# Attention and output projection as one pipeline over 24 blocks, with q and k split in the first projection

## The chip, the core and the metric

The kernel runs on one core of a Trainium2 chip. A core has TensorE (PE in the rows; its weight loads are listed apart as PEld), VectorE (DVE), ScalarE (ACT), GpSimd (POOL) and SyncE (SP), each with its own instruction stream. They wait for each other by semaphores. SP and POOL start the transfers between device memory and the two on-chip memories. The metric is the device time in microseconds; the median of the runs shown is what a change is measured against.

## What is computed

One encoder layer on 1024 + 2048 tokens of width 1024, in float32 (24 blocks of 128 tokens, block 8 starts the second sequence):

```python
h = rmsnorm(x, norm_mix)
z = h @ w_in                      # 1280 columns: 512 Fourier, 512 q, 128 k, 128 v
f = fourier_mix(z_f, w_fourier)   # 2-D DFT over positions and channels, then a 128x128 map per group
a = banded_attention(q, k, v)     # 8 query heads, 2 kv heads, 64 wide; keys of the blocks before, here, after
x = x + concat(f, a) @ w_out
h = rmsnorm(x, norm_ffn)
aff = softmax(h @ w_router)       # 16 experts; each takes its top 128 + 256 tokens
x = x + sum over experts of gate * ((silu(h @ w_gate) * (h @ w_up)) @ w_down)
y = rmsnorm(x, norm_final)
```

Attention of one query block: scores of at most 384 keys per head, plus a relative-position bias, softmax with one extra learned logit per head (the sink), times v.

## The kernel before, in words

A float32 product is made of three float32r products: each operand is split into a high part (a rounded copy, made by ACT) and a low part (operand minus high part, made by DVE), and `three_pass` (lines 103 to 107) adds hi·hi, hi·lo and lo·hi in PSUM. Where `pe.matmul` or `pe.transpose` is given plain float32, it is used whole; the trace shows such a matmul as two passes.

The stages run one after the other; between two of them all engines meet at a barrier.

1. `mixer_in` normalises x, multiplies by w_in in 6 chunks of 512 tokens, and stores z transposed (`zT`) and v by rows, both as float32.
2. `fourier` leaves f in the on-chip buffer `f_sb`, and stores it into `mixT`, in part from the next stage.
3. `attention` loops over the blocks. SP loads q and k of the next block, as float32. ACT makes their high parts (L771, L772), DVE q's low part (L818), and POOL k's low part (L733). q's high and low part lie one above the other on 128 partitions; a head's scores are one matmul with 128 rows (k_hi twice, L885) and one with 64 rows (k_lo, L886). DVE adds the bias and takes the maximum (L826), ACT takes the exponentials (L780), DVE divides (L847), PE transposes the probabilities in tiles of 128 keys (L897), ACT copies them out of PSUM (L762), PE multiplies by v (L904, 64 output rows, both kv heads into PSUM rows 0 to 63). The head outputs go to `mixT` in device memory. w_out is loaded and split beside this.
4. `mixer_out` loads each block of `mixT`, splits it (L1024, L1052), multiplies by w_out (48 matmuls of 512 columns a block), adds x (L1063), normalises (L1031 to L1070), stores h2 as a high and a low row of 4 KB each, transposes the block (L1106) and multiplies by the router weights (L1114). The logits are stored to device memory.
5. `routing` loads the logits and picks the tokens by a bisection on DVE.
6. `experts` loops over 16 experts, at 97 to 98 us each. Per expert, PE does the gate and up products (384 matmuls of 384 columns), transposes the gathered rows of the next expert, high and low part apart (L1611, 48 transposes of float32r), and does the down products (144 matmuls of 512 columns). ACT and DVE only copy the two transposed parts out of PSUM (L1472, L1517).
7. `final_norm`.

The order on each engine is written out by hand. Three limits matter below: PSUM has 8 banks of 512 columns; a waiting instruction holds up all that stand behind it on its engine; ACT, DVE and PE hand over to each other several times for each block.

Of the kernel before, what the change touches and what calls it, by code (L numbers as in the profile page):

```python
# [22 lines left out]
F32 = mybir.dt.float32  # L23
F32R = mybir.dt.float32r
# [7 lines left out]
P = 128  # L32
# [118 lines left out]
class SplitWeights:  # L151

    PIECES = 4

    def __init__(self, nc, kept, w):
        def sem(name):
            return kept.enter_context(nc.semaphore(f"wo_{name}"))

        self.KW = KT // self.PIECES
        self.raw = kept.enter_context(nc.sbuf_tensor("wo_raw", [P, 2, self.KW, D], F32))  # L160
        self.hi, self.lo = (kept.enter_context(nc.sbuf_tensor(f"wo_{n}", [P, KT, D], F32R)) for n in ("hi", "lo"))
        self.view = w.rearrange("(k p) n -> p k n", p=P)
        self.arrived, self.hi_done, self.lo_done = [sem("in0"), sem("in1")], sem("hi_done"), sem("lo_done")

    def load(self, sp, i):
        if i >= 2:
            sp.wait_ge(self.lo_done, i - 1)
        sp.dma_start(self.raw[:, i % 2], self.view[:, i * self.KW:(i + 1) * self.KW]).then_inc(self.arrived[i % 2], 16)

    def split_hi(self, act, i):  # L170
        act.wait_ge(self.arrived[i % 2], 16 * (i // 2 + 1))
        act.activation(self.hi[:, i * self.KW:(i + 1) * self.KW], self.raw[:, i % 2], ACT.Copy).then_inc(self.hi_done, 1)

    def split_lo(self, dve, i):
        ks = slice(i * self.KW, (i + 1) * self.KW)
        dve.wait_ge(self.hi_done, i + 1)
        dve.tensor_tensor(self.lo[:, ks], self.raw[:, i % 2], self.hi[:, ks].bitcast(F32), ALU.subtract).then_inc(self.lo_done, 1)

def mixer_in(nc, x, w_in, g_mix_cols, ident_d, rel_bias, bucket_rows, toeplitz, zT, v_rows):
# [4 lines left out]
    GRP = ZT + 1  # L186
    WP = 4
    ctx, sb, sem, ps = scope(nc, "p1")
    with ctx:
# [11 lines left out]
        z_sb = sb("z", [P, GRP, CW])  # L201
# [9 lines left out]
        zT_v = zT.rearrange("(t p) (c n) -> c t p n", p=P, n=CW)  # L211
        v_v = v_rows.rearrange("(c j p) d -> c p j d", p=P, j=CH)
        w_v = w_in.rearrange("(k p) n -> p k n", p=P)
        KW = KT // WP

        @block.sync
        def _(sp):
            sp.dma_start(ident[:, :], ident_d).then_inc(const_in, 16)
            sp.dma_start(g_col[:, :], g_mix_cols).then_inc(const_in, 16)
            bias_rows.load(sp, rel_bias, bucket_rows)  # L220
            for i in range(WP):
                if i >= 2:
                    sp.wait_ge(w_lo_done, i - 1)
                sp.dma_start(w_raw[:, i % 2], w_v[:, i * KW:(i + 1) * KW]).then_inc((w_in0, w_in1)[i % 2], 16)
            bias_rows.store(sp, toeplitz)
            with sp.Fori(0, NCH) as c:
                for g in range(GRP):
                    if g % 2 == 0:
                        sp.wait_ge(z_act, c * 5 + (g // 2 + 1))
                    else:  # L230
                        sp.wait_ge(z_dve, c * 5 + (g // 2 + 1))
                    if g < ZT:
                        sp.dma_start(zT_v[c, g], z_sb[:, g]).then_inc(stored, 16)
                    else:
                        sp.dma_start(v_v[c], z_sb[:, g].rearrange("p (j n) -> p j n", j=CH)).then_inc(stored, 16)
            sp.wait_ge(stored, 16 * GRP * NCH)
            sp.wait_ge(bias_rows.stored, 16)
# [9 lines left out]
        def _(act):  # L247
# [8 lines left out]
            def body(c, last):  # L256
# [5 lines left out]
                for g in range(0, GRP, 2):  # L262
                    if g == 0:
                        act.wait_ge(stored, c * (16 * GRP))
                    act.wait_ge(m_done, c * GRP + (g + 1))
                    act.activation(z_sb[:, g], ps[:, 4 + g % 4], ACT.Copy,
                                   scale=DH ** -0.5 if FW <= g * P < FW + QW else 1.0).then_inc(z_act, 1)
# [12 lines left out]
        def _(dve):  # L280
# [8 lines left out]
            def body(c, last):  # L289
# [7 lines left out]
                for g in range(1, GRP, 2):  # L297
                    if g == 1:
                        dve.wait_ge(stored, c * (16 * GRP))
                    dve.wait_ge(m_done, c * GRP + (g + 1))  # L300
                    dve.tensor_scalar(z_sb[:, g], ps[:, 4 + g % 4], DH ** -0.5 if FW <= g * P < FW + QW else 1.0,
                                      None, ALU.mult).then_inc(z_dve, 1)
# [15 lines left out]
        def _(pe):  # L318
# [3 lines left out]
            with pe.Fori(0, NCH) as c:  # L322
# [8 lines left out]
                for g in range(GRP):  # L331
                    bank = 4 + g % 4
                    if g < 4:
                        if g == 0:
                            pe.wait_ge(z_act, c * 5)
                            pe.wait_ge(z_dve, c * 5)
                    elif g % 2 == 0:
                        pe.wait_ge(z_act, c * 5 + (g - 4) // 2 + 1)
                    else:
                        pe.wait_ge(z_dve, c * 5 + (g - 4) // 2 + 1)  # L340
# [277 lines left out]
def attention(nc, zT, v_rows, attn_sink, ident_d, toeplitz, w_out, f_sb, mixT):  # L618

    ctx, sb, sem, ps = scope(nc, "p3")
    with ctx:
        ident = sb("ident", [P, P])
        bias = sb("bias", [P, NH, BAND])
        sink = sb("sink", [P, NH])  # L630
        q_raw, k_raw = sb("q_raw", [2 * DH, NH, P]), sb("k_raw", [2 * DH, NKV, BAND])
        q_split = sb("q_split", [2 * DH, NH, P], F32R)
        k_hi, k_lo = sb("k_hi", [2 * DH, NKV, BAND], F32R), sb("k_lo", [DH, NKV, BAND], F32R)
        v_sb = sb("v", [P, 3, KVW])
        s_sb, probs = sb("s", [P, NKV, GH, BAND]), sb("probs", [P, NKV, GH, BAND])
        mx, nm, es, esum, rs = (sb(n, [P, NKV, GH]) for n in ("mx", "nm", "es", "esum", "rs"))
        den = sb("den", [P, NKV, GH])
        gate = sb("gate", [P, NKV, GH])
        pt_sb = sb("pt", [P, NKV, 3, GH * P])
        o_sb = sb("o", [DH, NKV, GH * P])  # L640
        const_in, bias_in = sem("const_in"), sem("bias_in")
        f_stored = sem("f_stored")
        v_in, s_mm, added, t_mm, pt_done, pv_mm, o_out = (
            sem(n) for n in ("v_in", "s_mm", "added", "t_mm", "pt_done", "pv_mm", "o_out"))
        qk_hi_done, q_lo_done, k_lo_done = sem("qk_hi_done"), sem("q_lo_done"), sem("k_lo_done")
        qk_in, den_done = [sem(f"qk_in{kv}") for kv in range(NKV)], sem("den_done")
        stat, exp_done, normed = sem("stat"), sem("exp_done"), sem("normed")
        stored = [sem(f"stored{k}") for k in range(NKV)]
        block = ctx.enter_context(nc.Block())
        qT = zT[FW:FW + QW].rearrange("(h p) n -> p h n", p=DH)  # L650
        kT = zT[FW + QW:ZW].rearrange("(h p) n -> p h n", p=DH)
        o_v = mixT[FW:].rearrange("(v h p) (b n) -> v b p h n", v=NKV, p=DH, n=P)

        schedule, b = [], 0
        for s in SEQS:
            n = s // P
            final = b + n == TT  # L660
            schedule += [(b, b + 1, 2, 2 if b else 0, 3, 1, 0), (b + 1, b + 2, 3, 2, 3, 0, 0), (b + 2, b + n - 2, 3, 3, 3, 0, 0),
                         (b + n - 2, b + n - 1, 3, 3, 2, 0, 0), (b + n - 1, b + n, 2, 3, 0 if final else 2, 0, 1)]
            b += n

        def over_blocks(eng, body):


            for first, end, tiles, prev, after, at_start, next_at_start in schedule:
                lead, coming = 1 - at_start, (after, 1 - next_at_start)
                if end - first == 1:  # L670
                    body(first, tiles, prev, coming, lead)
                else:
                    with eng.Fori(first, end) as blk:
                        body(blk, tiles, prev, coming, lead)

        def wait(eng, sem_, value):
            if not isinstance(value, int) or value > 0:
                eng.wait_ge(sem_, value)


        N0 = SEQS[0] // P
        f_store_at = {0: 0, 1: 1, N0 + 1: 2, TT - 1: 3}

        def pieces(b, lag):

            at = {N0 - 2: (0,), N0 - 1: (1,), N0: (2,), TT - 2: (3,)}
            return at.get(b - lag, ()) if isinstance(b, int) else ()

        def split_cols(b):
            return slice(0, 2 * P if isinstance(b, int) and b == 0 else BAND)  # L690

        @block.sync
        def _(sp):
            sp.dma_start(ident[:, :], ident_d).then_inc(const_in, 16)
            sp.dma_start(sink[:, :], attn_sink.partition_broadcast(P)).then_inc(const_in, 16)
            def load_qk(b, tiles, lead):
                for kv in range(NKV):
                    wait(sp, q_lo_done, (b - 1) * NKV + kv + 1)
# [1135 lines left out]
```

## Time and profile before

| | |
|---|---|
| median of 3 runs | 3316.39 us (3312.01 to 3317.18) |
| profiled execution | span 3313.0 us from its first to its last instruction; no other time of it is given |
| PE busy | 2969.1 us, 90% of the span |
| DVE, ACT, POOL busy | 45%, 38%, 9% |
| first SP instruction of `attention` | 636.67 us |
| attention from the first score | 654 to 1096 us |
| output projection, from its first matmul to its last logits | 1113 to 1445 us |
| first SP instruction of `routing` | 1447.24 us |
| experts, first transposed row to last down product | 1546 to 3240 us |

Read the shares by stage: in the output projection and in the experts PE has no gap, in attention it has, and in the routing PE is nearly empty. "PEclk" is the share of full speed (2.4 GHz) that TensorE was granted: 1.00 is 2.4 GHz, 0.50 is 1.2 GHz, and a value between is a mean over a stretch that holds both.

### The profile page before, as it was taken

The page shows a single profiled execution, that of the slowest core. Times are in us where ns is not written, and L with a number is a line of the kernel's source. Part 1 is how long each engine was busy: PE and PEld are TensorE (multiplying, and loading weights), DVE is VectorE, ACT ScalarE, POOL GpSimd, SP SyncE. Part 2 cuts the span into 40 slices and gives each one's busy share as a digit, 9 for nine tenths or more (in the row PEclk, how much of TensorE's full clock was granted, in tenths as well). Part 3 has the DMA queues.
Part 4 walks back from the last instruction along what each step waited for, and adds up shares of the span by engine and source line. Part 5 has one row for each costly group of instructions (what it writes and reads, how often), then busy time and mean ns, then how long its engine had stood idle before and what let it go on. Part 6 is the DMA issues. An engine that isn't in the chain of part 4 may idle for free. (4 is left out here: it accounts for less than half of the span.)

```text
span 3313.0 us, 44990 instructions
## 1 busy us (share of the span) xinstructions
PE 2969.1 (90%) x15831; PEld 2527.0 (76%) x15831; DVE 1483.9 (45%) x2921; ACT 1248.4 (38%) x2103; POOL 308.5 (9%) x256
## 2 busy tenths in 40 slices
PE   7999968687899799944999999999999999999990
PEld 5888867543344588834999999999999999999990
DVE  3122147365555344456454444544444444544334
ACT  3121134365566233311343443433433443433334
POOL 0000000011111000000111111111101111111100
PEclk9999988888889899966999999999999999999995
DMA  5121124233222455542455455554545544555428
GB/s 164 64 85 73 42 79 139 65 99 105 79 82 85 135 192 196 195 155 83 157 174 184 143 161 171 177 160 143 177 157 173 183 146 149 174 184 153 151 78 302
DMA packets 252956, 464.88 MB, mean 140 GB/s; under 512 B 12491, under 2 KB 97644, under 8 KB 243180
## 3 DMA queue, kind: packets, MB, share of 16 engines
q1 hardware_dynamic: 225980, 367.71, 32.0%
q0 software_dynamic: 26928, 96.55, 11.3%
q8 instruction: 28, 0.46, 0.1%
q14 instruction: 20, 0.16, 0.0%
HBM read 358.11 MB, written 106.10 MB: 140 GB/s over the span
## 5 line engine op out<-in xcount | busy, mean ns | idle before, releaser
L1162 DVE TENSOR_TENSOR we_lo<-we_raw,we_hi 128x1024 fp32r<-128x1024 f32 x384 | 467.4, 1225 | 626.0 <-ACT we_hi L1157 625.4
L105 PE MATMUL p_psum<-p_xT_hi,we_hi 128*128 128x384 f32 x2048 | 692.9, 338 | 0.0
L107 PE MATMUL p_psum<-p_xT_hi,we_lo 128*128 128x384 f32 x2048 | 685.3, 335 | 0.0
L106 PE MATMUL p_psum<-p_xT_lo,we_hi 128*128 128x384 f32 x2048 | 685.0, 334 | 0.0
L1157 ACT ACTIVATE we_hi<-we_raw 128x1024 fp32r<-128x1024 f32 x384 | 400.0, 1051 | 6.0 <-DMA we_raw<-w_gate 5.8
L106 PEld LDWEIGHTS p_psum<-p_xT_lo,we_hi 128*128 128x128 f32 x2048 | 384.7, 188 | 0.6
L105 PEld LDWEIGHTS p_psum<-p_xT_hi,we_hi 128*128 128x128 f32 x2048 | 384.3, 188 | 0.6
L107 PEld LDWEIGHTS p_psum<-p_xT_hi,we_lo 128*128 128x128 f32 x2048 | 384.4, 188 | 0.0
L105 PE MATMUL p_psum<-we_hi,p_hid_hi 128*128 128x512 f32 x768 | 300.0, 391 | 0.0
L107 PE MATMUL p_psum<-we_hi,p_hid_lo 128*128 128x512 f32 x768 | 299.0, 389 | 0.0
L106 PE MATMUL p_psum<-we_lo,p_hid_hi 128*128 128x512 f32 x768 | 298.9, 389 | 0.0
L1501 ACT ACTIVATE p_y<-p_psum,p_gate_cur 128x512 f32<-128x512 f32 x96 | 66.0, 688 | 348.4 <-PE p_psum L107 217.5
L1476 ACT ACTIVATE p_hid_hi<-p_hid 128x384 fp32r<-128x384 f32 x128 | 67.2, 525 | 340.7 <-DVE p_hid L1564 340.7
L1486 ACT ACTIVATE p_sg<-p_psum 128x384 f32<-128x384 f32 x128 | 63.0, 493 | 287.7 <-PE p_psum L107 287.5
L1448 POOL DMA_INDIRECT x_left<-p_y,p_idx_cur x48 | 83.1, 1731 | 939.9 <-issue 862.2
L105 PE MATMUL p_psum<-p_h_hi,p_w_hi 128*128 128x512 f32 x432 | 169.2, 392 | 0.0
L106 PE MATMUL p_psum<-p_h_lo,p_w_hi 128*128 128x512 f32 x432 | 168.5, 390 | 0.0
L107 PE MATMUL p_psum<-p_h_hi,p_w_lo 128*128 128x512 f32 x432 | 168.3, 390 | 0.0
L105 PE MATMUL p_psum<-wo_hi,p_m_hi 128*128 128x512 f32 x384 | 155.2, 404 | 14.5 <-DVE p_m_lo L1052 14.5
L107 PEld LDWEIGHTS p_psum<-we_hi,p_hid_lo 128*128 128x128 f32 x768 | 144.1, 188 | 30.2
L106 PEld LDWEIGHTS p_psum<-we_lo,p_hid_hi 128*128 128x128 f32 x768 | 144.2, 188 | 29.6
L105 PEld LDWEIGHTS p_psum<-we_hi,p_hid_hi 128*128 128x128 f32 x768 | 144.1, 188 | 29.3
(213 smaller groups left out, 4610.8 us busy)
## 6 DMA issues: line engine op xcount, KB each, us to landing
we_raw<-w_gate SPq DMA_DIRECT2D x32, 2048.0 KB, 7.7
we_raw<-w_up SPq DMA_DIRECT2D x32, 2048.0 KB, 8.0
we_raw<-w_down SPq DMA_DIRECT2D x32, 2048.0 KB, 8.5
h<-p_h_split SPq DMA_DIRECT2D x24, 1024.0 KB, 3.9
zT<-p_z SPq DMA_DIRECT2D x54, 256.0 KB, 2.0
p_x<-x POOLq DMA_DIRECT2D x6, 2048.0 KB, 8.3
p_q_raw<-zT SPq DMA_DIRECT2D x96, 128.0 KB
p_m_raw<-mixT SPq DMA_DIRECT2D x24, 512.0 KB, 5.0
```

What stands on the lines that cost most here:

```text
L105: pe.matmul(out, lhi, rhi, start=first, stop=False)
L106: pe.matmul(out, lhi, rlo, start=False, stop=False)
L107: return pe.matmul(out, llo, rhi, start=False, stop=last)
L1157: act.activation(self.hi[:, n % self.HL, ks], self.raw[:, n % self.RAW, ks], ACT.Copy).then_inc(self.hi_done, 1)
L1162: dve.tensor_tensor(self.lo[:, n % self.HL, ks], self.raw[:, n % self.RAW, ks], self.hi[:, n % self.HL, ks].bitcast(F32), ALU.subtract).th ...
L1448: pool.indirect_dma_start(out=x2[half], out_offset=bass.IndirectOffsetOnAxis(ap=idx_cur[:, st:st + 1], axis=0), in_=y[:, st, :], in_offset ...
L1476: act.activation(hid_hi[:, half * FT + j], hid[:, j % 2], ACT.Copy).then_inc(hid_hi_done, 1)
L1486: act.activation(sg[:, j], ps[:, j, :SLOTS], ACT.Silu).then_inc(sg_done, 1)
L1501: act.activation(y[:, st], ps[:, 4 * half + st], ACT.Copy, scale=gate_cur[:, st]).then_inc(y_done[half], 1)
```

## The change

`mixer_in` writes q and k already split: ACT evacuates the high part of each of the 5 q and k tiles of a chunk, DVE the low part, and both go to device memory (`qk_parts`), 15 stores a chunk in place of 10.

`attention` and `mixer_out` become one function, `mixer`, without loops. Its steps s = -1 to 26 handle four blocks at a time: scores of block s+1, transposes and values of block s, the w_out products of block s-1, the norm and the transposes (`columns`) of block s-2, the router of block s-3. Scores are now two matmuls of 128 rows for each head (k_lo is loaded on both halves, too), in two PSUM banks in turn. The values of kv head 0 go to PSUM rows 0 to 63, those of kv head 1 to rows 64 to 127, and from there, split, straight into the w_out product; w_out's rows are reordered on the host to suit. x, h2 and others lie in `f_sb`, so ACT waits at its start until f of the second sequence is stored. 1/sqrt is taken as exp of a logarithm, x2 and h2 are stored by POOL, and the logits stay on chip for the routing.

h2 is one float32 row of 4 KB. The experts transpose it once (24 transposes of float32 in place of 48 of float32r), and the split is made from PSUM: ACT the high part, DVE the low part behind it.

```diff
@@ mixer_in, vector
+                for g in range(FG, ZT):
+                    dve.wait_ge(z_act, c * ACT_OUT + (FG // 2 + g - FG + 1))
+                    dve.scalar_tensor_tensor(out=qk_lo[:, g - FG], in0=ps[:, 4 + g % 4], scalar=scale_of(g),
+                                             in1=qk_hi[:, g - FG].bitcast(F32), op0=ALU.mult, op1=ALU.subtract).then_inc(z_dve, 1)
@@ mixer, sync: before the loop over blocks
+            load_qk(0)
...
+            load_qk(1)
+            load_v(0)
+            for i in range(2):
+                load_w(i)
+            load_f(0)
+            for g in range(FG):
+                store_f(sp, f_sb, f_stored, fT, 1, g)
@@ mixer, scalar
+            act.preload_act_table_set("natural_log_exp_and_others")
+            act.wait_ge(f_stored, 16 * FG)
+            act.wait_ge(eps_set, 1)
+            for s in STEPS:
+                if here(s):
+                    exps(s, 1)
+                if here(s - 1):
+                    heads_hi(s - 1)
+                if here(s):
+                    pt_out(s, 0)
+                if here(s - 2):
+                    norm(s - 2)
+                if here(s + 1):
+                    exps(s + 1, 0)
+                if here(s):
+                    pt_out(s, 1)
+                    channels_hi(s)
+                if here(s - 2):
+                    columns_out(s - 2, 0)
+                if here(s) and tiles[s] == 3:
+                    pt_out(s, 2)
+                if here(s - 2):
+                    columns_out(s - 2, 1)
@@ mixer, tensor
+                    pe.matmul(out, q_split[:, b % 2, h], k_hi[:, b % 2, kv, keys], start=True, stop=False)
+                    pe.matmul(out, q_split[:, b % 2, h], k_lo[:, b % 2, kv, keys], start=False, stop=True).then_inc(s_mm, 1)
...
+                    last = pe.matmul(ps[kv * DH:(kv + 1) * DH, 4], v_sb[:, b % 2, i, kv * DH:(kv + 1) * DH], pt_sb[:, i, kv],
+                                     start=i == 0, stop=i == tiles[b] - 1)
...
+            for s in STEPS:
+                scores(s + 1, (0, 1))
+                if here(s - 1):
+                    values(s - 1, tiles[s - 1] - 1)
+                    products(s - 1, 0, 0)
+                if here(s - 3):
...
+                    router(s - 3)
+                scores(s + 1, (2, 3))
+                if here(s):
+                    transposes(s, 0)
+                if here(s - 1):
+                    products(s - 1, 1, 0)
+                scores(s + 1, (4, 5))
+                if here(s):
+                    transposes(s, 1)
+                    values(s, 0)
+                if here(s - 1):
+                    products(s - 1, 0, 1)
+                if here(s - 2):
+                    columns(s - 2, 0)
+                scores(s + 1, (6, 7))
+                if here(s) and tiles[s] == 3:
+                    transposes(s, 2)
+                    values(s, 1)
+                if here(s - 1):
+                    products(s - 1, 1, 1)
+                if here(s - 2):
+                    columns(s - 2, 1)
@@ experts, vector
-                    dve.wait_ge(t_mm, e * (2 * KT) + 2 * k + 2)
-                    dve.tensor_copy(xT_lo[:, k], ps[:, (2 * k + 1) % 8, :SLOTS]).then_inc(x_lo_done, 1)
+                    dve.wait_ge(x_hi_done, e * KT + k + 1)
+                    dve.tensor_tensor(xT_lo[:, k], ps[:, k, :SLOTS], xT_hi[:, k].bitcast(F32), ALU.subtract).then_inc(x_lo_done, 1)
```

On PE, a stretch of the attention stage before: the four heads of one kv head (p_q_split is the weight, p_k_hi and p_k_lo stream), then the transposes of the probabilities and the values.

```order
L885 MATMUL p_psum<-p_k_hi,p_q_split 128x384
L886 MATMUL p_psum<-p_k_lo,p_q_split 128x384
L885 MATMUL p_psum<-p_k_hi,p_q_split 128x384
L886 MATMUL p_psum<-p_k_lo,p_q_split 128x384
L885 MATMUL p_psum<-p_k_hi,p_q_split 128x384
L886 MATMUL p_psum<-p_k_lo,p_q_split 128x384
L897 MATMUL p_psum<-p_ident,p_probs 128x128 x8
L904 MATMUL p_psum<-p_pt,p_v 64x512 x2
```

The same engine after the change, at the start of a step in the second sequence: two heads of the next block, the last values of the block before, and its first products with w_out (p_f_hi and p_f_lo are the Fourier channels, f_sb is the room that holds h2T).

```order
L940 MATMUL p_psum<-p_k_hi,p_q_split 128x384
L941 MATMUL p_psum<-p_k_lo,p_q_split 128x384
L940 MATMUL p_psum<-p_k_hi,p_q_split 128x384
L941 MATMUL p_psum<-p_k_lo,p_q_split 128x384
L961 MATMUL p_psum<-p_pt,p_v 64x512 x2
L105 MATMUL p_psum<-p_w_hi,p_f_hi 128x512
L106 MATMUL p_psum<-p_w_lo,p_f_hi 128x512
L107 MATMUL p_psum<-p_w_hi,p_f_lo 128x512
```

What stood in a stage of its own, the products, now stands between the links of attention's chain: 12 such rows follow each group of scores or values.

On DVE, attention before: the maximum of two heads (L826 with its read of the accumulator), the statistics (L836, L837), the normalisation of the block half behind (L844 to L847), and q's low part.

```order
L826 ISA p_s,p_mx<-p_psum,p_bias,p_sink 128x384
L826 ISA p_mx 128x1
L825 MEMSET p_gate 128x1
L826 ISA p_s,p_mx<-p_psum,p_bias,p_sink 128x384
L826 ISA p_mx 128x1
L836 TENSOR_SCALAR p_nm<-p_mx 128x4
L837 TENSOR_TENSOR p_es<-p_sink,p_mx 128x4
L844 TENSOR_TENSOR p_den<-p_rs,p_esum 128x4
L845 RECIPROCAL p_den<-p_den 128x4
L847 TENSOR_SCALAR p_probs<-p_s,p_den 128x384 x4
L818 TENSOR_TENSOR p_q_split<-p_q_raw,p_q_split 64x512
```

After, in the middle of a step: the statistics of block s+1, the logits of block s-3, the norm of block s-2 (L871 to L882, which waits for ACT), and then the next two heads of block s+1.

```order
L840 TENSOR_SCALAR p_nm<-p_mx 128x4
L841 TENSOR_TENSOR p_es<-p_sink,p_mx 128x4
L887 COPY lg<-p_psum 128x16
L871 TENSOR_SCALAR p_var<-p_ssq 128x1
L875 TENSOR_TENSOR p_newton<-p_rstd 128x1
L876 TENSOR_TENSOR p_newton<-p_newton,p_var 128x1
L877 TENSOR_SCALAR p_newton<-p_newton 128x1
L878 TENSOR_TENSOR p_rstd<-p_rstd,p_newton 128x1
L882 SCALAR_TENSOR_TENSOR f_sb<-f_sb,p_rstd 128x1024
L832 ISA p_s,p_mx<-p_psum,p_bias,p_sink 128x384
L832 ISA p_mx 128x1
```

The low part of q is gone, and the norm, which stood in the later stage, now stands ahead of the heads 4 and 5.

## Rows read from the trace of the kernel before

**Rows 1.** Busy time by stage: window, length, each engine's busy us, PEclk, DMA share, GB/s

```profile
654.00:1096.00 442.00, 378.76 (x1200) 180.11 (x1200) 251.55 (x1011) 266.25 (x713) 77.09 (x94) 0.87 0.31 90
...
1113.00:1450.00 337.00, 328.18 (x1719) 279.71 (x1717) 144.55 (x288) 103.53 (x144) 0.00 (x0) 0.98 0.52 182
...
1650.00:3112.00 1462.00, 1462.00 (x8591) 1371.16 (x8590) 674.71 (x838) 573.02 (x781) 190.48 (x123) 1.00 0.51 164
...
3240.00:3313.00 73.00, 0.00 (x0) 0.00 (x0) 39.16 (x90) 38.81 (x108) 0.00 (x0) 0.50 0.80 300
```

**Rows 2.** Waits in attention: who waited for whom, us in total, times, longest

```profile
ACT p_q_split L771 <- DMA p_k_raw<-zT: 72.6, 20, 11.7
...
PE p_psum L897 <- ACT p_pt L762: 30.4, 34, 2.6
```

**Rows 3.** PE in attention, in order of time: start, us, line, operation

```profile
1052.22 2.79 PE L904 MATMUL p_psum<-p_pt,p_v 128*64 128x512 f32 x6
1054.94 0.44 PE L885 MATMUL p_psum<-p_k_hi,p_q_split 128*128 128x384 f32 x1
1055.31 0.43 PE L886 MATMUL p_psum<-p_k_lo,p_q_split 64*128 64x384 f32 x1
...
1057.91 1.09 PE L897 MATMUL p_psum<-p_ident,p_probs 128*128 128x128 f32 x8
```

**Rows 4.** PE in the experts, in order of time

```profile
1699.80 0.33 PE L106 MATMUL p_psum<-p_xT_lo,we_hi 128*128 128x384 f32 x1
1699.97 0.33 PE L107 MATMUL p_psum<-p_xT_hi,we_lo 128*128 128x384 f32 x1
```

**Rows 5.** All engines in the output projection, in order of time: router, products

```profile
1333.12 1.85 PE L1114 MATMUL p_psum<-p_wr,p_h2T 128*128 128x16 f32 x16
...
1339.72 0.39 PE L105 MATMUL p_psum<-wo_hi,p_m_hi 128*128 128x512 f32 x1
...
1339.94 0.39 PE L106 MATMUL p_psum<-wo_lo,p_m_hi 128*128 128x512 f32 x1
```

**Rows 6.** PE in the output projection: the transposes of one block

```profile
1343.12 1.04 PE L1106 MATMUL p_psum<-p_ident,p_h 128*128 128x128 f32 x8
```

**Rows 7.** PE at the transposes of the gathered rows of one expert

```profile
2357.03 4.25 PE L1611 MATMUL p_psum<-p_ident,p_xe 128*128 128x128 f32 x48
2361.11 0.46 PE L105 MATMUL p_psum<-we_hi,p_hid_hi 128*128 128x512 f32 x1
```

**Rows 8.** Groups by line and shape, 400 to 1100 us: busy us, mean ns, idle before

```profile
L780 ACT ACTIVATE p_s<-p_s,p_nm 128x384 f32<-128x384 f32 x160 | 96.3, 606 | 5.1 <-DVE p_nm L836 5.1
L826 DVE CUSTOM_DVE_ANT_0 p_s<-p_psum,p_bias,p_sink 128x384 f32<-128x384 f32 x160 | 92.7, 614 | 3.6
...
L762 ACT ACTIVATE p_pt<-p_psum 128x512 f32<-128x512 f32 x136 | 76.2, 589 | 56.8 <-PE p_psum L897 56.8
...
L847 DVE TENSOR_SCALAR p_probs<-p_s,p_den 128x384 f32<-128x384 f32 x160 | 56.3, 416 | 1.4
```

**Rows 9.** Groups by line, 1000 to 1340 us: the norm

```profile
L1070 DVE SCALAR_TENSOR_TENSOR p_h<-p_x,p_rstd,p_gain 128x1024 f32<-128x1024 f32 x16 | 20.6, 1285 | 0.6
...
L1031 ACT ACTIVATE p_junk<-p_x 128x1024 f32<-128x1024 f32 x17 | 18.0, 1061 | 93.1 <-DVE p_x L1063 93.1
```

**Rows 10.** Busy time in stretches of 12 us, columns as in rows 1

```profile
640.00:652.00 12.00, 0.00 (x0) 0.00 (x0) 0.00 (x0) 1.87 (x4) 1.43 (x2) 0.50 0.66 182
...
808.00:820.00 12.00, 6.43 (x15) 3.82 (x16) 9.27 (x35) 3.83 (x8) 1.63 (x2) 0.61 0.52 163
```

**Rows 11.** SP's first instruction in attention

```profile
636.67 0.33 SPq L694 DMA_DIRECT2D p_ident<-identity  x1
```

**Rows 12.** Start of the routing, in order of time

```profile
1447.24 0.33 SPq L1218 DMA_DIRECT2D p_lg<-logits  x1
...
1451.69 0.23 DVE L1237 CAST p_same<-p_ranks 128x128 bf16<-128x128 f32 x1 [0.95 <-DMA p_ranks<-ranks]
```

**Rows 13.** The transposes of line 1611: PE's idle time before them, us and times

```profile
  DMA p_xe<-h,p_idx_next: 15.3, 1
```

More of the change, by code:

```diff
@@ L148, in store, with mixer_in @@
         sp.dma_start(toeplitz.rearrange("h (p n) -> p h n", n=NREL), self.rows[:, :]).then_inc(self.stored, 16)
[L151 to L181, printed above, removed]
+def mixer_in(nc, x, w_in, g_mix_cols, ident_d, rel_bias, bucket_rows, toeplitz, zT, qk_parts, v_rows):
     CH = 4
@@ L657, in attention @@
[L657 to L690, printed above, removed]
+        w_raw = sb("w_raw", [P, 2, KW, D])
@@ new lines, in mixer, with here @@
+        h_mm, h_out, lg_mm, lg_out = (sem(n) for n in ("h_mm", "h_out", "lg_mm", "lg_out"))
+        block = ctx.enter_context(nc.Block())
+        starts = (0, SEQS[0] // P)
+        ends = (SEQS[0] // P - 1, TT - 1)
+        tiles = [3 - (b in starts) - (b in ends) for b in range(TT)]
+        first = [b if b in starts else b - 1 for b in range(TT)]
+        before = [sum(tiles[:b]) for b in range(TT + 1)]
+        NEWTON = 4
+        STEPS = range(-1, TT + 3)
+        VERSIONS = NH * 2
+        def here(b):
+            return 0 <= b < TT
@@ L774, in exps @@
-            def exps(b, kv, tiles, behind):
-                for h in range(GH):
-                    if h == 2 and behind[2]:
-                        pt_out(*behind, range(2))
-                    wait(act, stat, (b * NKV + kv) * 2 + 1)
-                    act.activation(s_sb[:, kv, h, :tiles * P], s_sb[:, kv, h, :tiles * P], ACT.Exp, bias=nm[:, kv, h:h + 1],
-                                   accum_out=rs[:, kv, h:h + 1]).then_inc(exp_done, 1)
-                act.wait_ge(stat, (b * NKV + kv) * 2 + 2)
-                act.activation(esum[:, kv], es[:, kv], ACT.Exp).then_inc(exp_done, 1)
@@ L802, in _, with exps @@
-            split(0, 0)
-            split(0, 1)
-            split(1, 0)
-            over_blocks(act, body)
-            pt_out(TT - 1, 1, 2, range(2))
-            o_evac(TT - 1, 1)
+            def exps(b, half):
+                for h in range(half * HALF, (half + 1) * HALF):
+                    act.wait_ge(stat, (2 * b + half) * 2 + 1)
+                    scores = s_sb[:, b % 2, h, :tiles[b] * P]
+                    act.activation(scores, scores, ACT.Exp, bias=nm[:, b % 2, h:h + 1],
+                                   accum_out=rs[:, b % 2, h:h + 1]).then_inc(exp_done, 1)
+                heads = slice(half * HALF, (half + 1) * HALF)
+                act.wait_ge(stat, (2 * b + half) * 2 + 2)
+                act.activation(esum[:, b % 2, heads], es[:, b % 2, heads], ACT.Exp).then_inc(exp_done, 1)
@@ L864, in _, with add_max @@
-            first_tile = 0
-            for kv in range(NKV):
-                split(0, kv)
-            def band(head, tiles):
-                return bias[:, head, first_tile * P:(first_tile + tiles) * P]
-            over_blocks(dve, body)
-            normalise(TT - 1, 1, 2)
+            def add_max(b, heads):
+                for h in heads:
+                    dve.wait_ge(s_mm, b * NH + h + 1)
+                    if b >= 2:
+                        dve.wait_ge(t_mm, before[b - 1] * NKV)
+                    at = 0 if first[b] < b else P
+                    dve.tensor_tensor_reduce(
+                        out=s_sb[:, b % 2, h, :tiles[b] * P], in0=ps[:, h % 2, :tiles[b] * P],
+                        in1=bias[:, h, at:at + tiles[b] * P], scale=1.0, scalar=sink[:, h:h + 1],
+                        op0=ALU.add, op1=ALU.max, accum_out=mx[:, b % 2, h:h + 1]).then_inc(added, 1)
@@ L874, in _ @@
         @block.tensor
         def _(pe):
-            pe.wait_ge(const_in, 32)
-            def scores(b, kv, tiles):
-                u = b * NKV + kv
-                pe.wait_ge(q_lo_done, u + 1)
-                pe.wait_ge(k_lo_done, u + 1)
-                for h in range(GH):
-                    wait(pe, added, (u - 1) * GH + (h + 1))
-                    out, head, keys = ps[:, h, :tiles * P], kv * GH + h, slice(0, tiles * P)
-                    pe.matmul(out, q_split[:, head], k_hi[:, kv, keys], start=True, stop=False)
-                    pe.matmul(out, q_split[:DH, head], k_lo[:, kv, keys], start=False, stop=True).then_inc(s_mm, 1)
@@ L908, in body, with scores @@
[L908 to L914 removed]
+            def scores(b, heads):
+                if not here(b):
+                    return
+                if heads[0] == 0:
+                    pe.wait_ge(qk_in[b % 2], 96 * (b // 2 + 1))
+                keys = slice(0, tiles[b] * P)
+                for h in heads:
+                    if b * NH + h >= 2:
+                        pe.wait_ge(added, b * NH + h - 1)
+                    out, kv = ps[:, h % 2, keys], h // GH
+                    pe.matmul(out, q_split[:, b % 2, h], k_hi[:, b % 2, kv, keys], start=True, stop=False)
+                    pe.matmul(out, q_split[:, b % 2, h], k_lo[:, b % 2, kv, keys], start=False, stop=True).then_inc(s_mm, 1)
@@ new lines, in transposes @@
+            def transposes(b, i):
+                if i == 0:
+                    pe.wait_ge(normed, (b + 1) * NH)
+                for kv in range(NKV):
+                    done = (before[b] + i - 1) * NKV + kv + 1
+                    if done > 0:
+                        pe.wait_ge(pt_done, done)
+                    for h in range(GH):
+                        last = pe.transpose(ps[:, 2 + kv, h * P:(h + 1) * P], s_sb[:, b % 2, kv * GH + h, i * P:(i + 1) * P], ident[:, :])
+                    last.then_inc(t_mm, 1)
@@ new lines, in columns, with router @@
+            def columns(b, half):
+                if half == 0:
+                    pe.wait_ge(h2_done, b + 1)
+                    if b:
+                        pe.wait_ge(lg_out, b)
+                else:
+                    pe.wait_ge(h_out, 2 * b + 1)
+                for k in range(4):
+                    at = (half * 4 + k) * P
+                    last = pe.transpose(ps[:, 7, k * P:(k + 1) * P], h2_sb[b % 2][:, at:at + P], ident[:, :])
+                last.then_inc(h_mm, 1)
+            def router(b):
+                pe.wait_ge(h_out, 2 * b + 2)
+                for k in range(KT):
+                    last = pe.matmul(ps[:, 7, :NE], h2T[:, k * P:(k + 1) * P], wr[:, k], start=k == 0, stop=k == KT - 1)
+                last.then_inc(lg_mm, 1)
@@ L1166, with routing @@
 PAY = 5
[L1169 removed]
+def routing(nc, lg, ranks_d, ident_d, weights, pos_m, payload, onehot_row):
     ctx, sb, sem, ps = scope(nc, "p5")
```

705 lines of the change are left out of this document (310 added, 395 removed).

## Prediction

> **What bounds the kernel now.** I read the busy time by stage first. In the experts PE is busy for all of 1462 us at clock 1.00, in the output projection for 328.18 of 337 us at 0.98, in attention for 378.76 of 442 us at 0.87 [rows 1]. So only attention has idle time to give, 63.2 us; elsewhere only fewer or shorter PE instructions help. The waits of attention come next: 72.6 us is ACT on the load of q and k, 30.4 us is PE on ACT's copy of the transposed probabilities [rows 2]; the second is a hand-over from PE to ACT and back with nothing to do between. DVE and ACT work 251.55 and 266.25 of the 442 us there [rows 1], so neither bounds. The reader should then look at PE in order of time [rows 3 to 7], start to start, for the price of one instruction.
>
> **The change on PE, piece by piece.** (Start to start, near full clock.)
> - Scores. In attention 128-row and 64-row matmuls alternate, 0.37 us each (1054.94 to 1055.31) [rows 3]; in the experts, where all have 128 rows, one of 384 columns takes 0.17 (1699.80 to 1699.97) [rows 4]. The new ones have 128 rows. Bounds 0.17 and 0.37; I take 0.173, the row with the same shape: 20 blocks x 16 x 0.173 = 55.4, and 4 end blocks of two tiles, 16 x 0.14 each, 9.0.
> - Values: 1052.22 to 1054.94 is 2.72 us for three instructions of two passes each [rows 3], 0.907 an instruction; 68 tiles x 2 = 136 of them, 123.4.
> - Transposes of float32: eight take 1.04 with a latency of some 0.27 in it, so 0.11 each [rows 6]. 544 of probabilities 59.8, 192 of h 21.1.
> - Products: 0.227 each (1339.72 to 1339.94 is 0.22; a block's mean is the bit more) [rows 5]; 24 x 48 make 261.2. Router 1.85 a block [rows 5], 44.4.
>
> Sum 574 us, at clock 1.00; at the projection's 0.98 it would be 586. A full step is 2.8 + 2.6 + 5.4 + 10.9 + 1.9 + 0.9 = 24.5 us. To this come some six changes between kinds of work in a step, among them those to and from the values, which use 64 output columns; no row holds one alone. Eight transposes next to scores and values last 1.09 us, 0.05 more than eight among full-size work [rows 3, 6]; each alternating score costs 0.20 more than the experts' [rows 3, 4]. Between these I take 0.16, nearer to the scores, which change the size of the weight too: 1 us a step, 24 in all; bounds 0 and 1.2 a step.
>
> A place where a rule and the trace can be compared: alternating 128 and 64 rows costs 0.37 against 0.17 [rows 3, 4]. The Trainium skill ("TensorEngine Tiling (Array Packing)", section Key Properties) says "Mode switching requires drain". That agrees with the two rows; and it speaks against the change where the values (128 rows, 64 columns) still stand six times a step between full-size work. By it the 1 us a step stays; without it the sum would be 24 us less.
>
> **The stage as a whole.** Before, attention and projection take 1447.24 - 636.67 = 810.6 us from SP's first instruction to the routing's [rows 11, 12]. After:
> - (a) ACT's first exponential waits until f is stored, and that store stands on SP behind q, k, bias, v, half of w_out and f: 10.6 MB by their shapes. At 182 GB/s [rows 10] that is 58 us, at 300 (the final norm's) [rows 1] 35; I take 44, between. Nothing hides it: behind ACT's wait stand all its exponentials, so DVE and PE wait too, after the scores of two blocks.
> - (b) From there to the first transposes of block 1, latency counts: on ACT three halves of exponentials (4 x 0.606 each) and then a fourth, four splits of 2048 columns of w_out (two Squares' length, 2.1 each), three copies of 0.6, on DVE two normalisations (4 x 0.416), transposes 0.9 [rows 6, 8, 9]: 9.7 + 8.4 + 1.8 + 3.3 + 0.9 = 24, with hand-overs 28. Bounds 20 and 40.
> - (c) The rest of PE's work, 574 less 13 that (a) and (b) hold, and the 24: 585.
> - (d) After the last product: residual, Square 1.06, the rest of the norm 2.4, transposes, copy, router, logits, the meeting of the engines; in part in PE's sum. 8; bounds 4 and 12.
>
> 44 + 28 + 585 + 8 = 665; saved 145.6.
>
> **Why (c) should hold without waits.** I laid a full step of 25.5 us out, in the written order. PE: heads 0, 1 at 0, last values 0.7, products 2.5, router 5.2, heads 2, 3 at 7.1, transposes 0 at 7.8, products 8.7, heads 4, 5 at 11.4, transposes 1 at 12.1, values 13.0, products 14.8, columns 17.5, heads 6, 7 at 18.0, transposes 2, values, products 21.3, columns 24.1. DVE's work in it: 8 x 0.614 + 8 x 0.416 + 6 copies or sums of 512 columns at 0.6 + 1.285 and small ones, about 14 us; ACT's: 8 x 0.606 + 10 copies at 0.589 + 1.06 and small ones, about 13 [rows 8, 9]. With these the probabilities of heads 4 to 7 are normalised at 5.4 and needed at 7.8; the first transposes are copied at 9.9 and their bank is needed at 12.1; h2 is ready at 14.1 and needed at 17.5; heads 4, 5 are off their banks at 15.2 and needed at 18.0. So each hand-over has 2.2 to 3.4 us, and the 30.4 us of PE's wait in attention [rows 2] has products to stand under. Load waits: q and k come a whole block ahead, already split, and ACT's 72.6 us of waiting [rows 2] goes.
>
> **Other edits.** In the experts 48 transposes take 2357.03 to 2361.11, 4.08 us [rows 7]; 24 of float32 at 0.11 take 2.64; 15 x 1.44 = 21.6 saved, since PE has no gap there [rows 1]. DVE's subtraction now follows ACT's copy; 1462 - 674.71 us of DVE idle time covers it. The first gather moves half the bytes: PE waits 15.3 us for it now [rows 13]; between 0 and half (7.7) is saved, I take 2.4, nearer to 0, since the choice of tokens and the start of the transfer don't shrink. The logits' trip: DVE starts in the routing on another load at 1451.69, 4.45 us after the stage's start [rows 12], so 0.4 is saved there. `mixer_in`: a group of 24 products of 512 columns takes PE 5.4 us; one more DVE pass of 0.6 and the added store (0.26 MB, 1.4 us at 182 GB/s) hide beside it; 0, bounds 0 and +3.
>
> **The sum.** 145.6 + 21.6 + 2.4 + 0.4 = 170 less: 3313.0 - 170 = 3143 us of span. The median shown is 3.4 us above the span, so 3146. Its own bounds: (a) -9/+14, (b) -8/+12, the changes of work -24/+5, the clock +12, gather -5/+2; taken together as independent some -30/+30: 3116 to 3176.
>
> **Rivals.**
> 1. The values of the two kv heads overlap. They now go to different halves of the output columns. In a pair, four passes of 0.45 would take the time of three: 68 x 0.45 = 31 us less, 3115; if two, 61 less, 3085. For it: nothing in PE's row depends on the other head. Against it: before, both stood in the same half, so no row shows two halves side by side, and both need all 128 rows. The Trainium skill (the same page and section) says that different tiles can load weights and multiply in parallel, which is this rival. 20 in 100.
> 2. The margins of 2.2 to 3.4 us fail, as a hand-over costs more than its parts (DVE and ACT each have some ten waits in a step, in a fixed order, and one that is late moves the rest). Then what attention had of idle time stays: 63 us more, 3209. For it: attention had the waits though DVE and ACT were idle for 40% of it [rows 1]. Against it: twice as much PE work now stands between the links. 22 in 100.
> 3. The scores stay at 0.37 us in spite of 128 rows, because each loads new weights behind a wait for a bank: 20 x 16 x 0.197 + 64 x 0.11 = 70 more, 3216. Against it: the experts' row is also a new weight each [rows 4]. 6 in 100.
> 4. The change does not do what it says: the two chains block each other, and a step takes 442/24 + 337/24 = 32.5 us as before [rows 1]. Stage time 780 + 30, all but the experts' gain lost: some 3290 to 3315, no change at the upper end. 2 in 100.
> 5. Slower: PE gets short idle stretches in every step and its granted clock falls with them. The stretch 808 to 820, where PE is busy 6.43 of 12 us, has 0.61, between the two levels of 1.2 and 2.4 GHz, the projection without gaps 0.98 [rows 1, 10]. At a mean clock m the 574 us become 574/m; the 170 are gone at m = 574/744 = 0.77; at 0.70 it is 246 more, 3392. Against it: the step has nearly as little idle time as the projection. 3 in 100.
>
> **Numbers.** The forecast has 47 in 100. The range reaches over it to rival 1 with one pass saved and on the other side to rivals 2 and 3: 3095 to 3215; outside lie rival 1 at two passes, the longer half of 2 and 3, and 4 and 5, some 18 in 100. The measurement cannot tell 0.2%, 6.6 us, from no change. Faster 0.95 (the forecast and rivals 1 to 3), same 0.02 (rival 4), slower 0.03 (rival 5).
>
> **What would show it.** In the new profile: the first exponential some 44 us after SP's first instruction of the stage (term a); then a period of 25 to 26 us between the values' or the scores' instructions of successive blocks, with PE busy above 95% and a clock near 1.00 (c; rivals 2, 4, 5); scores 0.17 apart (rival 3); the values' two instructions of a tile 0.9 apart, not 0.45 or 0.68 (rival 1); the routing some 665 us after the stage's start; expert transposes 2.6 us long, and experts 1.4 us shorter each. The forecast is wrong if PE waits over 2 us a step on ACT or DVE, or if the stage's start takes much over 72 us.

## The result, and the profile after

The changed kernel takes 3076.65 us (median of 4 runs, 3075.53 to 3078.93), 0.928 of the kernel before (95% interval 0.9266 to 0.9292). That is 240 us less; 170 were forecast, and the time lies below the range. The profiled execution's span is 3073.8 us, 239.2 less than before, and it divides so:

| part | before | after | saved | forecast |
|---|---|---|---|---|
| up to SP's first instruction of the stage | 636.7 | 634.8 | 1.9 | 0 |
| attention and projection, to the routing's first SP instruction | 810.6 | 599.8 | 210.7 | 145.6 |
| routing, to the first transposed row of the experts | 99.0 | 96.4 | 2.5 | 2.8 |
| experts and final norm | 1766.8 | 1742.7 | 24.1 | 21.6 |

Before, the four marks are 636.67, 1447.24, 1546.20 (PE's first transpose of gathered rows) and the span's end; after, 634.80, 1234.64, 1331.06 and the end. Only the second row is far off. The marks of that stage, in order of time, from the changed kernel's trace (they answer to [rows 11, 12]):

```profile
634.80 0.73 SPq L676 DMA_DIRECT2D p_q_split<-qk_hi  x1
...
671.10 0.51 ACT L752 ACTIVATE p_s<-p_s,p_nm 128x256 f32<-128x256 f32 x1 [35.01 <-DMA fT<-f_sb]
...
1226.95 1.11 PE L991 MATMUL p_psum<-p_ident,f_sb 128*128 128x128 f32 x4 [2.49 <-DVE f_sb L882]
...
1234.64 0.34 SPq L1144 DMA_DIRECT2D p_ident<-identity  x1
```

ACT's first exponential comes 36.3 us after SP's first instruction, released by the store of f. The first transposes of block 1 start at 702.99. The steady part ends at 1221.2, and what comes then is the norm and the router of the last block, with waits. The stage by stretches (window, length, each engine's busy us, PEclk, DMA share, GB/s), to be held against [rows 1]:

```profile
660.00:680.00 20.00, 1.62 (x4) 1.14 (x4) 6.60 (x14) 7.83 (x20) 0.00 (x0) 0.50 0.53 209
680.00:700.00 20.00, 12.03 (x43) 7.92 (x44) 16.44 (x47) 11.84 (x26) 0.00 (x0) 0.68 1.10 274
700.00:1200.00 500.00, 500.00 (x2719) 383.72 (x2717) 280.51 (x942) 257.12 (x703) 35.07 (x65) 1.00 0.51 142
1200.00:1234.00 34.00, 29.45 (x150) 23.89 (x148) 8.44 (x20) 7.59 (x16) 3.77 (x7) 0.87 0.20 78
```

From 700 to 1200 PE is never idle and its clock is 1.00, where attention had 63 idle us and a clock of 0.87. DVE and ACT are busy for 56% and 51%. The waits of PE between 710 and 1200 are an empty list; the 30.4 us on the copies [rows 2] are gone. One steady step, PE in order of time (start, us, line, operation), which answers to [rows 3, 5, 6]:

```profile
860.00 0.33 PE L940 MATMUL p_psum<-p_k_hi,p_q_split 128*128 128x384 f32 x1
860.17 0.34 PE L941 MATMUL p_psum<-p_k_lo,p_q_split 128*128 128x384 f32 x1
...
860.70 1.03 PE L951 MATMUL p_psum<-p_ident,p_s 128*128 128x128 f32 x8
861.67 1.08 PE L961 MATMUL p_psum<-p_pt,p_v 128*64 128x512 f32 x4
862.68 0.50 PE L105 MATMUL p_psum<-p_w_hi,p_o_hi 128*128 128x512 f32 x1
863.01 0.39 PE L106 MATMUL p_psum<-p_w_lo,p_o_hi 128*128 128x512 f32 x1
...
874.62 1.85 PE L997 MATMUL p_psum<-p_wr,f_sb 128*128 128x16 f32 x16
...
897.45 1.85 PE L997 MATMUL p_psum<-p_wr,f_sb 128*128 128x16 f32 x16
```

The scores are 0.17 us apart, as taken. The router's starts are 22.83 us apart, a step; 25.5 were forecast. Most of the difference stands in one row: the values of a tile, both kv heads, four passes, take 861.67 to 862.68, 1.01 us. The forecast had 1.81, and a step has three of them: 2.4 of the 2.7 us.

In the experts, the transposes of one expert:

```profile
2129.66 2.78 PE L1531 MATMUL p_psum<-p_ident,p_xe 128*128 128x128 f32 x24
2132.20 0.47 PE L105 MATMUL p_psum<-we_hi,p_hid_hi 128*128 128x512 f32 x1
```

2.54 us instead of 4.08 [rows 7]; 2.64 was forecast.

### The profile page after: what moved, and what is told of

The parts are those of the page before. It is cut to its first block and busy times, and to the rows that moved or that the text cites. A ratio compares the mean times of both kernels' runs of the same rounds, so it can differ in the third digit from the quotient of the medians.

```text
span 3073.8 us, 41939 instructions
## 1 busy us (share of the span) xinstructions
PE 2779.8 (90%) x15447; PEld 2459.1 (80%) x15447; DVE 1410.9 (46%) x2675; ACT 1160.4 (38%) x2017; POOL 268.9 (9%) x233
## 5 line engine op out<-in xcount | busy, mean ns | idle before, releaser
L832 DVE CUSTOM_DVE_ANT_0 p_s<-p_psum,p_bias,p_sink 128x384 f32<-128x384 f32 (+1 forms) x192 | 106.7, 592 | 161.7 <-PE p_psum L941 161.7
```

The costliest lines, as they stand in the source:

```text
L832: dve.tensor_tensor_reduce(out=s_sb[:, b % 2, h, :tiles[b] * P], in0=ps[:, h % 2, :tiles[b] * P], in1=bias[:, h, at:at + tiles[b] * P], sc ...
```

## The experiments

All medians stand against 3076.65 us, or 3077.21 us in the run `after_again`, which is the changed kernel once more beside the later ones.

> The changed kernel once more, beside the others on the same chip, so that their differences of some 10 us can be read: 3077, 0.928 of the kernel before.

3077.21 us (5 runs), 0.9285 (0.9273 to 0.9298). Each of the two ratios is good to some 4 us, so differences of some 6 us can be read.

**1. What is short about the values? (`probe_halves`)** An added stage between the mixer and the routing issues rows of matmuls on zeros, with products of full size ahead of each row. It ran once, and only the rows inside that execution are read:

```diff
+            for i in range(24):
+                pe.matmul(ps[lo, 0], w[:, lo], m[:, :], start=True, stop=True)
...
+            for i in range(12):
+                pe.matmul(ps[lo, 0], w[:, lo], m[:, :], start=True, stop=True)
+                pe.matmul(ps[up, 0], w[:, up], m[:, :], start=True, stop=True)
```

> The changed kernel with an added stage behind the mixer, which only measures TensorE: rows of float32 matmuls of 512 columns with 64 output columns (a) all into PSUM rows 0 to 63 of one bank, (b) the same in two banks in turn, (c) in turn into rows 0 to 63 and 64 to 127 of one bank, as the changed values are, (d) the two halves in two banks, (e) two of one half, then two of the other, (f) 128 output columns, (g) pairs of 128-row matmuls of 384 columns against (h) 128 rows and 64 rows in turn, (i) values and float32r products in turn. Theory A (two column halves side by side overlap): a 0.91 us an instruction, b 0.91, c and d about 0.45 to 0.50, e between, about 0.68. Rival B (an instruction is short now because consecutive ones do not add into the same PSUM rows or bank): b is as short as d, 0.5, and c lies with a or b. Rival C (nothing to do with the halves, the instruction itself is now 0.5): a is 0.5 too. g 0.17 and h 0.37 if the alternation of row counts is what cost 0.20.

PE in order of time in the added stage. L1062 is row (a), L1065 (b), L1068 and L1069 (c), L1077 and L1079 (e), L1082 (f), L1092 and L1093 (h), L1096 and L1097 (i); L1058 are the products between the rows:

```profile
1278.13 20.81 PE L1062 MATMUL pp_psum<-pp_m,pp_w 128*64 128x512 f32 x48
1298.87 3.01 PE L1058 MATMUL pp_psum<-pp_mr,pp_wr 128*128 128x512 f32 x12
1301.81 20.81 PE L1065 MATMUL pp_psum<-pp_m,pp_w 128*64 128x512 f32 x48
1322.56 3.01 PE L1058 MATMUL pp_psum<-pp_mr,pp_wr 128*128 128x512 f32 x12
...
1328.12 0.59 PE L1068 MATMUL pp_psum<-pp_m,pp_w 128*64 128x512 f32 x1
1328.13 0.59 PE L1069 MATMUL pp_psum<-pp_m,pp_w 128*64 128x512 f32 x1
1328.56 0.59 PE L1068 MATMUL pp_psum<-pp_m,pp_w 128*64 128x512 f32 x1
1328.56 0.59 PE L1069 MATMUL pp_psum<-pp_m,pp_w 128*64 128x512 f32 x1
...
1358.35 0.59 PE L1077 MATMUL pp_psum<-pp_m,pp_w 128*64 128x512 f32 x1
1358.41 0.59 PE L1079 MATMUL pp_psum<-pp_m,pp_w 128*64 128x512 f32 x1
...
1365.66 10.46 PE L1082 MATMUL pp_psum<-pp_m,pp_w 128*128 128x512 f32 x24
...
1404.48 0.45 PE L1092 MATMUL pp_psum<-pp_mr,pp_wr 128*128 128x384 f32 x1
1404.86 0.44 PE L1093 MATMUL pp_psum<-pp_mr,pp_wr 64*128 64x384 f32 x1
...
1413.33 1.07 PE L1096 MATMUL pp_psum<-pp_m,pp_w 128*64 128x512 f32 x2
1414.33 0.49 PE L1097 MATMUL pp_psum<-pp_mr,pp_wr 128*128 128x512 f32 x1
1414.75 1.07 PE L1096 MATMUL pp_psum<-pp_m,pp_w 128*64 128x512 f32 x2
```

In one half, 24 instructions of two passes take 20.7 us, 0.86 each, in one bank (a) or in two (b). In the two halves a pass of the one starts with a pass of the other, 0.01 us apart, and the next pair 0.43 us later (c); in two banks it is the same (d). So the two halves run wholly side by side, and the bank has no part in it: theory A holds, B falls with row (b) and C with row (a). Row (e), two of one half and then two of the other, was expected between; its passes pair up just as well, 0.06 us apart. A full 128 columns (f) take 0.43 a pass, too, from start to start within the row. So a matmul into 64 columns costs what one of 128 costs, and its other half is free for a matmul into that half that stands close behind it (c to e). A product of full size does not use it: in row (i) one instruction of 64 columns and one product in turn take 1.42 us (1413.33 to 1414.75), more than the 0.86 and 0.23 that they take each among their like. Row (h), 128 and 64 rows in turn, is 0.37 apart, against 0.17 for 128 rows alone (g).

**2. The same in the kernel (`values_apart`).**

```diff
-                for kv in range(NKV):
...
-                last.then_inc(pv_mm, 1)
+                one(0)
+                late.append(lambda: one(1).then_inc(pv_mm, 1))
```

`one(kv)` is the same matmul; what stands in `late` is issued behind the next three products. Block 0's first tile has no products behind it and keeps its pair, so 67 of the 68 tiles are parted.

> The changed kernel, but the matmul of kv head 1 stands three products behind that of kv head 0 instead of next to it; same work, same output. Theory A (halves overlap only side by side): each takes 0.91 us again, and two more changes of kind at 0.1 each come to each of 68 tiles: 68 x (1.81 + 0.2 - 1.01) = 68 us slower, 3145. Rivals B and C (the halves are not it): only the changes, some 14 us slower, 3090.

3158.55 us (3156.7 to 3160.19), 82 us slower: theory A, 14 above its number. PE in order of time (L964 are the values here):

```profile
866.14 1.07 PE L964 MATMUL p_psum<-p_pt,p_v 128*64 128x512 f32 x2
867.15 0.50 PE L105 MATMUL p_psum<-p_w_hi,p_o_hi 128*128 128x512 f32 x1
867.49 0.39 PE L106 MATMUL p_psum<-p_w_lo,p_o_hi 128*128 128x512 f32 x1
867.72 0.40 PE L107 MATMUL p_psum<-p_w_hi,p_o_lo 128*128 128x512 f32 x1
868.04 1.07 PE L964 MATMUL p_psum<-p_pt,p_v 128*64 128x512 f32 x2
869.05 0.50 PE L105 MATMUL p_psum<-p_w_hi,p_o_hi 128*128 128x512 f32 x1
```

One kv head alone takes 1.01 us (866.14 to 867.15), as long as both together in the changed kernel. To this comes 0.1 us on each side (867.15 to 867.49 and 867.72 to 868.04 in place of 0.23), so 1.2 us a tile; 67 tiles make 81. PE was busy without a gap from 720 to 1280, at clock 1.00.

**3. The scores' second matmul back at 64 rows (`scores_64_rows`).**

```diff
-                    pe.matmul(out, q_split[:, b % 2, h], k_lo[:, b % 2, kv, keys], start=False, stop=True).then_inc(s_mm, 1)
+                    pe.matmul(out, q_split[:DH, b % 2, h], k_lo[:DH, b % 2, kv, keys], start=False, stop=True).then_inc(s_mm, 1)
```

> The changed kernel with the second scores matmul back at 64 rows (k_lo on q's high part alone, as in the kernel before), so that 128 and 64 rows alternate. If the term of the scores was right (0.37 instead of 0.173 us), 20 x 16 x 0.2 + 64 x 0.11 = 71 us slower, 3148. If the alternation was not what cost the time in attention before (the wait for the bank was, say), no change, 3077.

3168.33 us (3151.07 to 3171.98), 92 us slower, against 71. In the trace the scores stand 0.37 us apart again:

```profile
882.33 0.44 PE L940 MATMUL p_psum<-p_k_hi,p_q_split 128*128 128x384 f32 x1
882.70 0.44 PE L941 MATMUL p_psum<-p_k_lo,p_q_split 64*128 64x384 f32 x1
```

So the term of the scores is confirmed. Beside it stands a lower clock. The steady part by stretches:

```profile
720.00:1290.00 570.00, 570.00 (x2632) 397.75 (x2631) 280.77 (x918) 252.34 (x680) 35.16 (x65) 0.95 0.44 121
```

PE has no idle time, and still 0.95 was granted; 5% of 570 us is 28. That this makes up the other 21 us is an estimate from the one profiled execution (3171.98 us), and no run holds the clock apart.

**4. The same part alone in the kernel before (`before_scores_128`).**

```diff
-        k_hi, k_lo = sb("k_hi", [2 * DH, NKV, BAND], F32R), sb("k_lo", [DH, NKV, BAND], F32R)
+        k_hi, k_lo = (sb(n, [2 * DH, NKV, BAND], F32R) for n in ("k_hi", "k_lo"))
...
-                    pe.matmul(out, q_split[:DH, head], k_lo[:, kv, keys], start=False, stop=True).then_inc(s_mm, 1)
+                    pe.matmul(out, q_split[:, head], k_lo[:, kv, keys], start=False, stop=True).then_inc(s_mm, 1)
```

> The kernel before with one part of the change alone: k_lo is made on both halves, and the second scores matmul has 128 rows (lo x lo is added too). Theory (the row counts in turn cost 0.2 us each): 24 x 16 x 0.2 = 75 us of PE time go in attention; of them those that stand where PE waited anyway come back as waits, so 30 to 75 us faster, 3235 to 3280. Rival (attention before was bound by its chain of hand-overs and the loads): the time goes into waits, under 15 us faster.

3324.14 us against 3313.71 of the kernel before beside it, 1.003 (1.0019 to 1.0041): nothing gained, some 10 us lost, the rival. Attention by stretches, which answers to the first row of [rows 1]:

```profile
654.00:1096.00 442.00, 312.18 (x1178) 172.63 (x1178) 245.87 (x997) 261.85 (x705) 75.56 (x92) 0.84 0.30 90
```

and PE's waits there (what waited for what, us, times, longest), the first answering to [rows 2]:

```profile
PE p_psum L897 <- ACT p_pt L762: 90.0, 39, 5.7
```

PE is busy 66.6 us less (378.76 to 312.18), and idle 66.6 us more; its wait for the copies alone grew from 30.4 to 90.0. What is worth 92 us in the pipeline is worth nothing where PE waits.

**5. The products in one place (`products_in_one_place`).**

```diff
                     products(s - 1, 0, 0)
+                    products(s - 1, 1, 0)
+                    products(s - 1, 0, 1)
+                    products(s - 1, 1, 1)
...
                 if here(s):
                     transposes(s, 0)
-                if here(s - 1):
-                    products(s - 1, 1, 0)
...
```

> The changed kernel with the four product groups of a step in one place, behind the last values of the block before, instead of one behind each link of attention's chain; the same instructions. Theory (the products are the cover of the hand-overs): in the other part of the step PE has only 8 us of work beside 3.6 us of copies, 4.8 of exponentials and Square on ACT and some 8 us on DVE, so PE waits 4 to 6 us in a step: 22 x 5 = 110 us slower, 3190. Rival (the waits of attention before were those for the loads and the split of q and k, which are gone anyway): under 20 us slower.

3189.61 us (3184.8 to 3190.63), 112 us slower: the number of the theory, but not quite by its waits. The steady part by stretches, and then PE's waits in it:

```profile
720.00:1300.00 580.00, 519.05 (x2614) 387.14 (x2613) 272.79 (x924) 248.78 (x688) 35.09 (x65) 0.95 0.44 120
```

```profile
PE p_psum L991 <- DVE f_sb L882: 39.2, 21, 2.0
PE p_psum L105 <- DVE f_sb L866: 18.9, 20, 1.3
...
PE p_psum L951 <- ACT p_pt L763: 0.2, 1, 0.2
```

61 us of idle time, and a clock of 0.95 (5% of 580 us is 29): some 90 of the 112 us; the rest is not divided. PE waits for h2 (L882) and for the sum with x that frees the products' banks (L866), not for the copies of the probabilities: 0.2 us. So the products do cover hand-overs, and the late one without them is the norm's; that attention's own links need this cover was argued, and this run does not show it.

**6. The start (`no_wait_at_start`, `loads_ahead`).** First ACT's wait alone is taken out:

```diff
-            act.wait_ge(f_stored, 16 * FG)
```

> The changed kernel without ACT's wait for the stored f at the head of its stream; all that writes f_sb's room still comes after loads that SP starts behind that wait. Theory (the store holds up the start, 36.3 us to the first exponential, behind nothing else): the first exponential some 18 us earlier, when the first four maxima are there (652), and the stage 10 to 18 us shorter, 3059 to 3067; the loads of block 2, which SP issues behind the same wait, limit it. Rival (the transfers as a whole bound the start, the wait only marks it): PE waits for the loads of w_out and of block 2 instead, under 5 us gained.

3067.26 us (3066.6 to 3069.59), 0.9267 (0.9253 to 0.9281): 9 us faster by the medians, 4 by the ratios, which is too little for the ratios to tell. In the traces the stage takes 589.0 us (636.55 to 1225.53) in place of 599.8, which is the theory's lower edge. The first exponential came at 653.9, 17 us earlier, as the theory said, but PE then stood 11.9 us for k of block 2, as the rival said; SP issues these loads behind its own wait for f. So, with the order of the loads changed as well:

```diff
             load_f(0)
+            load_qk(2)
+            load_v(1)
+            load_f(1)
+            for i in range(2, 4):
+                load_w(i)
             for g in range(FG):
                 store_f(sp, f_sb, f_stored, fT, 1, g)
-            for i in range(2, 4):
-                load_w(i)
...
             sp.wait_ge(f_stored, 16 * FG)
+            load_x(0)
...
-            for s in range(TT):
+            for s in range(1, TT):
```

> The changed kernel without ACT's wait for the stored f, and with SP's order changed: q, k, v and f of the blocks 1 and 2 and the last halves of w_out are loaded before f is stored. In the run without the wait alone PE stood 11.9 us for k of block 2, which SP had issued at 677.4 behind the wait for f. Theory: with that gone the steady steps begin some 20 us earlier than in the changed kernel (680 in place of 700), 3057 on the first chip, 10 less than without the wait alone. Rival (the 10 MB themselves are the bound, in whatever order): x of block 0 is late instead, DVE holds up, and it is within 4 us of the run without the wait.

3058.4 us (3058.11 to 3060.22), 0.9232 (0.922 to 0.9245) against 0.9285 of the changed kernel beside it: 19 us faster, and the fastest of all here. The stage takes 580.0 us (636.28 to 1216.24). The stretch that was 12.03 us busy at 0.68 before (680 to 700):

```profile
680.00:700.00 20.00, 19.39 (x96) 14.73 (x95) 11.79 (x37) 10.35 (x31) 0.55 (x1) 0.98 0.94 275
```

The steady steps begin 20 us earlier, and the transfers, at 275 GB/s, are no bound for them.

## Why the prediction was wrong

**The step that failed** is the first list's term of the values, "0.907 an instruction; 68 tiles x 2 = 136 of them, 123.4". It summed two instructions as if they ran one behind the other; they run side by side. A pair takes 1.01 us with the changes, 0.80 less than 1.81; of the 68 tiles, 66 lie behind 702.99, 53 us. Rival 1 had the mechanism and its size in its second form (two passes, 61 us, 3085), but I gave all of it 20 in 100, and ended the range at 3095, between its two forms. Neither sign that the prediction names for being wrong came (waits over 2 us a step, a start over 72 us); what told was the sign of rival 1, the spacing of the values. The reason against it, that both heads need all 128 rows, was no reason: probe (c) shows that they don't exclude each other. The sentence of the Trainium skill ("TensorEngine Tiling (Array Packing)", Key Properties), that different tiles load weights and multiply in parallel, agrees with the probe: 0.86 us for two instructions in two halves, as much as for one alone.

The other terms:
- Term (a), the store of f: 36.3 us, 44 forecast. It hangs on the store, as said: without the wait the exponentials come 17 us earlier. (Before that wait PE gets through the scores of one block, not of two.) Term (b), to the first transposes of block 1: 31.9, 28 forecast; the wait for k of block 2 (6.7 us) was not in it. Together 4 us better than forecast.
- Term (c), the rest of PE's work: 518.2 us (702.99 to 1221.2), 585 forecast. The values are 53 of these 67. The transposes take 0.09 to 0.10 us each in place of 0.11, some 10 over the stage. The router's 1.85 was the length of its row; from start to start it takes 1.70 (874.62 to 876.32), some 3 over the stage. The products take 0.232 in place of 0.227, 6 more. And some 5 of the forecast's work in (c), the last routers and transposes, ran behind 1221.2, in (d). A step holds ten changes of kind, at 0.09 to 0.18 each: 1.1 a step, 1 forecast.
- Term (d), the end: 13.4 us (1221.2 to 1234.64), 8 forecast, at clock 0.50 from 1226 to 1234: the last router takes 3.60 us there, not 1.85.
- The scores, 0.173: right (0.17), and scores_64_rows shows what it is worth.
- That (c) holds without waits: right. Rivals 2, 4 and 5 fall with PE's empty list of waits and the clock of 1.00; rival 3 with the scores' rows.
- Experts 24.1 of 21.6 (16 transposed sets of 1.5 us, the first among them), gather and logits' trip 2.5 of 2.8, `mixer_in` 0 as far as can be seen: right.

So the stage gave 211 us and the rest 28, where 146 and 24 were forecast: 53 of the 69 are the values, 10 the transposes, and the rest is small.

## What to carry to other kernels

Two float32 matmuls of 64 output columns that go to different halves cost as much as one of them when they stand next to each other in PE's queue, and more than twice that when products of full size stand between (1.0 and 2.2 us a tile). A cheaper PE instruction is worth its full price where PE never waits (71 us by the rows, 92 measured) and nothing where it does (the same edit in the kernel before), so first ask which of the two a stage is. When a stage starts with a store that only a later step needs, put the wait at that step and the loads ahead of the store: 19 us here.

## What the runs showed of the hardware

- TensorE's granted clock can be lower though the profile shows no idle time. With 128 and 64 rows in turn (scores_64_rows) PE had no gap in 570 us and the clock was 0.95, a mean of the levels of 1.2 and 2.4 GHz; with the values apart, nearly as much time added and no gap either, it was 1.00. In the probe's row (h) it fell within the row: up to 1405.2 the clock is 1.00 and the matmuls are 0.37 us apart, from there to 1410 it is 0.51 and they are 0.62 apart. In row (i), 64 columns and a product in turn, it was 1.00 (1413 to 1425). What of the alternating rows lowers it, no run shows.

```profile
1405.23 0.66 PE L1092 MATMUL pp_psum<-pp_mr,pp_wr 128*128 128x384 f32 x1
1405.81 0.69 PE L1093 MATMUL pp_psum<-pp_mr,pp_wr 64*128 64x384 f32 x1
1406.43 0.69 PE L1092 MATMUL pp_psum<-pp_mr,pp_wr 128*128 128x384 f32 x1
```

- A change from matmuls of 64 columns to full-size ones costs 0.1 us (0.33 in place of 0.23 between the first two products behind the values), half of what 128 and 64 rows in turn cost for each instruction (0.20).
